# Sample attention with key pages turned in place on VectorE, all 128 score rows in use, and prompt units with one PSUM bank of each kind

## The chip, the cores and the metric

One core of a Trainium2 chip runs the whole kernel. The metric is the device time of one execution in microseconds, median of several runs. Engines are TensorE (PE), VectorE (DVE), ScalarE (ACT), GpSimd (POOL) and SyncE (SP), which issues nearly all DMAs.

## The reference, cut to what matters

The reference is one step of a two-layer decoder: a gated linear recurrence with a mixture of experts, then differential attention with a second mixture of experts, for 512 prompt tokens and 8 sequences of 4 new tokens. Only the attention of the second layer is touched. Its part for the 8 sequences, which read 16 cached pages of 128 keys each:

```python
qs = (q.astype(F32) * B_DH ** -0.5).reshape(DB, T, B_HEADS, 2, B_DH)     # 8 x 4 x 8 heads x 2 halves x 64
for p in range(n_pages):                                                  # 16 pages through page_table
    kp = cache_k[page_table[:, p]].reshape(DB, PAGE_SIZE, B_HEADS, 2, B_DH)
    vp = cache_v[page_table[:, p]]
    s = jnp.einsum('bthcd,bkhcd->bhctk', qs, kp) + alibi(p * PAGE_SIZE + jnp.arange(PAGE_SIZE))
    # running softmax over all pages and the 4 new keys, weights times vp
out = o[:, :, 0] - lam * o[:, :, 1]                                       # the two halves of a head
```

The prompt part is the same with 512 queries and keys and a causal mask: for each head and each block of 128 queries two score rows (halves c = 0, 1), a softmax of each, `a = p[:, :, 0] - lam * p[:, :, 1]`, and `a @ v`. Everything is float32. The result goes through a norm per head and the weights `b_w_o`.

## The kernel before

Layers are stages; a stage is a few blocks, in which every engine has an instruction list written out by hand, held together by semaphores. There is no scheduler: the order in the lists is the order of the code.

**kvq_block (L1575)** projects keys, queries and values from weights in `wring`, a ring of three tiles of 2 MB. Its queries are written twice, as `qT[0]` and `qT[1]`, each with the other half's 64 rows cleared (L1671, two memsets of 64x4352). SyncE loads the two halves of `b_w_o` (4.2 MB) at its end, into ring slots that nothing else then uses.

**prompt_attention (L1734)** runs 32 units, eight heads times four query blocks; unit i of a head has width 128 (i + 1). A unit is: two score matmuls (L1779), a bias with a maximum on VectorE (`bias_max`, L1831, negated in L1836), two exponentials on ScalarE (L1863), a combination with lambda on VectorE (`combine`, L1843 to L1846), transposes of the weights (L1789), their copy on ScalarE (L1871), the value matmuls (L1798), and two copies out on ScalarE (L1877, L1879). Scores, turned weights and values have two PSUM banks each (four for the scores, for two halves). TensorE works two units ahead with the scores and one behind with the values; VectorE and ScalarE work one unit ahead:

```python
bias_max(0)
for n in range(N):
    if n + 1 < N:
        bias_max(n + 1)
    combine(n)
```

GpSimd makes the bias of each head (L1769) when the one two heads before has been used. Four key pages of the first sequence are loaded meanwhile (L1730).

**sample_attention (L1894)** is a loop over the sequences: iteration b scores sequence b and takes the values of sequence b - 1. A key page (128 keys on partitions, 1024 columns of 8 heads) is turned on TensorE by eight 128x128 transposes (L2097) into two PSUM banks, ScalarE copies one bank out (L1990), VectorE the other (L2057). Four turned pages are a group of 512 keys, scored by 8 matmuls with 32 output rows each (L2115), of which 16 are in use. Values need 8 matmuls a group (L2147). The key pages have four slots in one ring tile, the value pages eight in a tile of their own; SyncE asks for a page when its slot is free. At the end of a sequence come a maximum, one exponential of 128x2052, the scaling of the weights, and `own`/`place`, which pick each head's rows and add them to the output.

**mix_out_block (L909)** then norms the output, turns it and multiplies by `b_w_o`.

## Time and profile before

| what | value |
|---|---|
| median of 3 runs | 1841.38 us (1836.94 to 1850.53) |
| the profiled execution | 1837.61 us, its span 1835.8 us |
| mean granted TensorE clock | 0.899 |
| TensorE busy | 1427.6 us (78% of the span) |
| VectorE, ScalarE, GpSimd busy | 703.8, 420.7, 151.6 us |
| read and written in DRAM | 303.37 MB and 47.84 MB |

The span is the time from the first to the last instruction in the profile; the small rest of an execution lies around it. A busy share is an average over stages with different limits, so the rows shown further down are taken by stage.

### The profile page before, as it was taken

What the parts mean: (1) busy time and instruction counts of PE and PEld (TensorE: products, weight loads), DVE (VectorE), ACT (ScalarE), POOL (GpSimd) and SP (SyncE); (2) the same over time, 40 slices, a digit from 0 to 9 for tenths busy, and PEclk for the clock granted to TensorE, in tenths of its full rate; (3) what the DMA queues carried; (4) which work ended last, traced back from release to release, by engine and by line L of the source; (5) the groups of instructions that cost most, each with busy time, mean ns of one, the idle gap of its engine ahead of it and who ended that gap; (6) DMA issues with size and microseconds to landing.
All of it is one profiled execution on the core that took longest, in us unless ns stands there. A gap on an engine that the chain in (4) does not pass through costs nothing. (4 is left out here: it accounts for less than half of the span.)

```text
span 1835.8 us, 28081 instructions
## 1 busy us (share of the span) xinstructions
PE 1427.6 (78%) x10387; PEld 816.1 (44%) x10387; DVE 703.8 (38%) x1752; ACT 420.7 (23%) x984; POOL 151.6 (8%) x174
## 2 busy tenths in 40 slices
PE   4998888986782998539989687888888769469980
PEld 2445454564441655224444454544444424245540
DVE  4225554467442111161001684344444443511115
ACT  2023343333110111030110573222222201111111
POOL 1002232222002000110000110000000000100002
PEclk9999989997895999869989898899999989679995
DMA  5133142223603999811311206999999861179974
GB/s 187 46 120 105 51 142 94 76 95 116 220 0 123 335 360 350 277 58 46 123 64 46 101 1 232 386 372 363 376 379 368 338 234 83 43 258 377 347 238 155
DMA packets 133580, 352.74 MB, mean 192 GB/s; under 512 B 22220, under 2 KB 52095, under 8 KB 125152
## 3 DMA queue, kind: packets, MB, share of 16 engines
q1 hardware_dynamic: 117108, 320.81, 48.5%
q0 software_dynamic: 4992, 17.83, 2.7%
q10 hardware_dynamic: 11372, 12.62, 2.1%
q8 instruction: 73, 1.20, 0.3%
q14 instruction: 35, 0.29, 0.0%
HBM read 303.37 MB, written 47.84 MB: 191 GB/s over the span
## 5 line engine op out<-in xcount | busy, mean ns | idle before, releaser
L431 PE MATMUL bank<-wring,xT 128*128 128x512 f32 x768 | 354.5, 622 | 22.6 <-ACT gla_fin L551 16.1
L431 PEld LDWEIGHTS bank<-wring,xT 128*128 128x128 f32 x768 | 152.1, 201 | 212.2 <-issue 192.5
L2097 PE MATMUL bank<-ident,wring 128*128 128x128 f32 x1024 | 141.9, 292 | 30.9 <-DMA wring<-cache_k 22.0
L2097 PEld LDWEIGHTS bank<-ident,wring 128*128 128x128 f32 x1024 | 122.2, 150 | 65.7 <-issue 42.5
L1990 ACT ACTIVATE sa_kT<-bank 128x512 f32<-128x512 f32 x128 | 76.5, 597 | 219.2 <-PE bank L2097 219.2
L2057 DVE COPY sa_kT<-bank 128x512 f32<-128x512 f32 x128 | 87.9, 691 | 72.5 <-PE bank L2097 72.4
L798 PE MATMUL bank<-xT,wring 128*128 128x512 f32 x256 | 111.9, 595 | 0.0
L798 PEld LDWEIGHTS bank<-xT,wring 128*128 128x128 f32 x256 | 48.1, 190 | 59.3 <-issue 59.3
L2147 PE MATMUL bank<-sa_v,sa_at 128*32 128x512 f32 x512 | 64.7, 624 | 8.5 <-DMA sa_v<-cache_v 7.1
L706 DVE COPY_PREDICATED gla_att<-level_masks,bank 128x512 f32<-128x512 int32 x48 | 35.1, 730 | 91.2 <-PE bank L818 91.2
L2115 PE MATMUL bank<-sa_kT,sa_q 128*32 128x512 f32 x512 | 62.7, 607 | 3.5 <-DVE sa_kT L2057 3.5
L2019 DVE CUSTOM_DVE_ANT_0 sa_scores<-bank,sa_alibi 128x512 f32<-128x512 f32 (+1 forms) x40 | 23.2, 580 | 93.3 <-issue 93.3
L818 PE MATMUL bank<-gla_qe,gla_ke 128*128 128x128 f32 x384 | 52.5, 295 | 4.7 <-DVE gla_att L706 4.7
L1632 PE MATMUL bank<-attn_q_xT,wring 128*128 128x512 f32 x128 | 55.7, 594 | 0.0
L322 PE MATMUL bank<-ident,attn_o 128*128 128x128 f32 (+1 forms) x80 | 11.7, 300 | 54.3 <-DVE attn_o L411 43.7
L818 PEld LDWEIGHTS bank<-gla_qe,gla_ke 128*128 128x128 f32 x384 | 49.2, 206 | 7.7 <-DVE gla_att L706 7.0
L1779 PE MATMUL bank<-attn_kT,attn_qT 128*128 128x128 f32 (+3 forms) x128 | 42.9, 462 | 10.5 <-PEq L1609 8.5
L1677 DVE COPY attn_v<-bank 128x512 f32<-128x512 f32 (+1 forms) x16 | 7.8, 488 | 96.4 <-PE bank L431 93.9
L584 ACT ACTIVATE gla_diff<-gla_diff 128x512 f32<-128x512 f32 (+1 forms) x48 | 30.3, 632 | 60.5 <-DVE gla_diff L674 51.5
L1450 PE MATMUL bank<-moe_wgu,hgrn_g 128*64 128x256 f32 x352 | 43.0, 400 | 1.2 <-DVE hgrn_g L1386 1.2
L1450 PE MATMUL bank<-moe_wgu,moe_area 128*64 128x256 f32 x352 | 42.6, 397 | 1.2 <-DVE moe_area L1386 1.2
L1435 PE MATMUL bank<-ident,hgrn_g 96*128 96x96 f32 x128 | 14.7, 261 | 36.6 <-DMA hgrn_g<-slots_x 36.6
(374 smaller groups left out, 2053.5 us busy)
## 6 DMA issues: line engine op xcount, KB each, us to landing
wring<-cache_k SPq DMA_DIRECT2D x128, 512.0 KB, 5.8
sa_v<-cache_v SPq DMA_DIRECT2D x128, 512.0 KB, 5.6
moe_wd<-moe_w_down SPq DMA_DIRECT2D x32, 1024.0 KB, 15.4
moe_wgu<-moe_w_gate SPq DMA_DIRECT2D x22, 1024.0 KB, 12.0
moe_wgu<-moe_w_up SPq DMA_DIRECT2D x22, 1024.0 KB, 13.6
wring<-a_w_in SPq DMA_DIRECT2D x16, 1024.0 KB, 8.8
slots_x<-gla_vm SPq DMA_DIRECT2D x27, 384.0 KB, 5.6
wring<-moe_w_gate SPq DMA_DIRECT2D x10, 1024.0 KB, 14.7
```

The lines of the kernel that those rows point to most:

```text
L431: last = nc.tensor.matmul(bank[:, :], xT[:, c, cols(t)], w[:, c, :], start=(c == 0), stop=(c == DC - 1))
L706: nc.vector.copy_predicated(A[:, :, :], bcast(k.levelmask[:, i, :].bitcast(I32), 1, [P, PT, P]), k.ps[3 + i % 2][:, :].rearrange("p (c n) ...
L798: last = nc.tensor.matmul(bank[:, :], lhsT, k.xT[:, c, 0:SEQ], start=(c == 0), stop=(c == DC - 1))
L818: last = nc.tensor.matmul(k.ps[3 + i % 2][:, part], KE[i][:, part], QE[i][:, part], start=True, stop=True)
L1450: nc.tensor.matmul(out, XT[u][:, c, 0:WIDE], WGU[s][:, :, c, n * P:(n + 1) * P], start=(c == 0), stop=(c == DC - 1))
L1632: last = nc.tensor.matmul(bank[:, :], w[:, c, (h % 4) * P:(h % 4 + 1) * P], q_xT[:, c, 0:SEQ], start=(c == 0), stop=(c == DC - 1))
L1779: last = nc.tensor.matmul(k.ps[2 * (n % 2) + c][:, 0:w], qT[c][:, h, i * P:(i + 1) * P], kT[:, h, 0:w], start=True, stop=True)
L1990: nc.scalar.activation(KT[:, 0:half, (p % GROUP) * P:(p % GROUP + 1) * P], k.ps[2 * (p % 2)][:, :].rearrange("p (h n) -> p h n", h=half), ...
L2057: nc.vector.tensor_copy(KT[:, half:HEADS, (p % GROUP) * P:(p % GROUP + 1) * P], k.ps[2 * (p % 2) + 1][:, :].rearrange("p (h n) -> p h n", ...
L2097: last = nc.tensor.transpose(k.ps[2 * (p % 2) + n][:, h * P:(h + 1) * P], K[:, p % KRING, hh * P:(hh + 1) * P], k.ident[:, :])
L2115: last = nc.tensor.matmul(k.ps[4][QUAD * j:QUAD * (j + 1), 0:w], Q[:, h, :], rhs, start=(n == 0), stop=(n == 1))
L2147: last = nc.tensor.matmul(k.ps[5 + n][QUAD * q:QUAD * (q + 1), :], AT[:, p, :], rhs, start=(p < 4), stop=(p == PAGES or (p >= PAGES - 3)))
```

## The change

1. **One block for both attentions.** `prompt_attention` and `sample_attention` become `attention_block` (L1754), with slots s from -32 to 36. The prompt units have the slots -32 to -1, the key groups (four pages) the slots 0 to 31, and the value group v_s = s - 5 is taken in slot s. The loops are written out; there is no loop in the instruction lists any more.
2. **Prompt units with one bank of each kind.** Two banks for the scores (one for each half), one for turned weights, one for values. In a slot TensorE does the scores of unit n + 1, then turns and values of unit n; VectorE does the combination of unit n and then the bias of n + 1. The halves are contracted over 64 rows each, so `qT` is written once and nothing of it is cleared. The division by the sum moves from the combination into ScalarE's copy of the values; the large scaling L1845 goes, a 128x1 multiply comes.
3. **Keys turned in place.** VectorE turns a page in its own SBUF tile as 4 x 32 blocks of 32x32 (STREAM_TRANSPOSE, 128x1024). A partition then holds a quarter of the keys and one of 32 features. The queries are spread to `Q`, in which each quarter of the partitions has its own eight columns, so that the 32 output rows of a matmul are four quarters x 2 halves x 4 tokens, and four matmuls over the feature chunks add up. All 128 score rows are in use, with 512 columns in two banks' halves for 16 pages. 32 matmuls of 32x128 score a group, in place of 32 transposes of 128x128 and 8 matmuls of 32x512, and the two evictions of a page go.
4. **Preparation and end of a sequence.** GpSimd clears tiles and spreads the queries (16 copies of 32x8x2x4 ahead of the first bias, 48 behind the last). TensorE spreads the queries and scores all new keys first. At the end of a sequence there are two exponentials of 128x512, some 20 small VectorE instructions that take the maximum and sum over the four quarters, and 16 small copies of the turned weights on ScalarE in place of VectorE's five reductions.
5. **Loads.** Keys and values have two groups of four pages each; the keys in two ring tiles, the values in the third and in `xT`. Key group 0 is loaded in kvq_block, group 1 at the start of attention_block. `b_w_o` moves from kvq_block to behind the last key group.

```diff
 def kvq_block(k, a, kv_xT, q_xT, ks, v, kT, qT, kTs, qs, smp_q, keys):
...
             sp.wait_ge(out_v, 2 * NT)
             store(ks, "k_prompt", "k_sample")
-            for i in range(2):
-                k.load_weights(sp, column_halves(a["b_w_o"][0], i * HB))
+            sp.wait_ge(done, count[("q", HEADS - 1)])
+            sp.wait_ge(keys.table_in, 16)
+            keys.place()
+            for p in range(GROUP):
+                keys.load_k(sp, 0, p)
...
+def attention_block(k, a, rep, v, kT, qT, kTs, qs, o_s, keys):
...
+                for s in SLOTS_S:
+                    if 1 <= s < STEPS:
+                        if s >= 2:
+                            sp.wait_ge(scored, s - 1)
+                        for r in range(GROUP):
+                            keys.load_k(sp, s, r)
+                    v_s = s - LAG
+                    if s == STEPS + 1:
+                        sp.wait_ge(scored, STEPS)
+                        for i in range(2):
+                            k.load_weights(sp, column_halves(a["b_w_o"][0], i * HB))
+                    if v_s >= 0:
+                        if v_s >= 2:
+                            sp.wait_ge(valued, v_s - 1)
+                        for r in range(GROUP):
+                            keys.load_v(sp, v_s, r)
...
+                def p_scores(n):
...
+                        if n:
+                            pe.wait_ge(p_biased, 2 * n)
+                        rows_c = slice(c * half, (c + 1) * half)
+                        nc.tensor.matmul(P_SCORE[c][:, 0:w], qT[rows_c, h, i * P:(i + 1) * P], kT[rows_c, h, 0:w],
+                                         start=True, stop=True).then_inc(p_scored, 1)
...
+                def score(s):
+                    b, g = s // GROUPS_, s % GROUPS_
+                    pe.wait_ge(keys_turned, GROUP * (s + 1))
...
+                    for n in range(2):
+                        for i in range(GROUPS_):
+                            for j in range(4):
+                                h = 2 * j + n
...
+                                last = nc.tensor.matmul(out.rearrange("p (r x) -> p r x", r=GROUP), Q[b % 2][:, h, i, :],
+                                                        keys.K[s % 2][:, :, at:at + QUAD], start=(i == 0), stop=(i == GROUPS_ - 1))
+                    last.then_inc(scored, 1)
...
+                def turn_page(s, r):
+                    dve.wait_ge(keys.k_in[s % 2 * GROUP + r], 16 * (s // 2 + 1))
+                    page = keys.K[s % 2][:, r, :]
+                    nc.vector.transpose(page, page).then_inc(keys_turned, 1)
...
+                for s in SLOTS_S:
...
+                    for n in units_at(s):
+                        p_combine(n)
+                    if 0 <= s < STEPS:
+                        turn_page(s, 0)
...
+                    for n in units_at(s + 1):
+                        p_bias_max(n)
```

In the order of VectorE's list before, in the prompt attention, the bias step of width 512 (L1831, L1836) stands ahead of the combination of width 384 (L1843 to L1846):

```order
L1831 ISA xT,pa_stat<-bank,pa_bias 128x512
L1831 ISA pa_stat 128x1
L1831 ISA xT,pa_stat<-bank,pa_bias 128x512
L1831 ISA pa_stat 128x1
L1836 TENSOR_SCALAR pa_stat<-pa_stat 128x2
L1843 RECIPROCAL pa_stat<-pa_stat 128x2
L1844 TENSOR_TENSOR pa_stat<-pa_stat,row_gains 128x1
L1845 TENSOR_SCALAR xT<-xT,pa_stat 128x384
L1846 SCALAR_TENSOR_TENSOR xT<-xT,pa_stat 128x384
```

The same engine and place now (`pa_s` holds the scores and weights, `pa_stat` the maxima and sums):

```order
L2031 RECIPROCAL pa_stat<-pa_stat 128x2
L2032 TENSOR_TENSOR pa_stat<-pa_stat 128x1
L2033 TENSOR_TENSOR pa_stat<-pa_stat,row_gains 128x1
L2034 SCALAR_TENSOR_TENSOR pa_s<-pa_s,pa_stat 128x384
L2020 ISA pa_s,pa_stat<-bank,pa_bias 128x512
L2020 ISA pa_stat 128x1
L2020 ISA pa_s,pa_stat<-bank,pa_bias 128x512
L2020 ISA pa_stat 128x1
L2024 TENSOR_SCALAR pa_stat<-pa_stat 128x2
```

The combination of the unit of width 384 now stands ahead of the bias step of the unit of width 512, which was behind it.

TensorE's list before, in the prompt attention, from the turn of the unit of width 256 on: L1779 are scores, L1789 transposes of the weights, L1798 values.

```order
L1789 MATMUL bank<-ident,xT 128x128 x2
L1798 MATMUL bank<-attn_v,pa_at 128x128
L1779 MATMUL bank<-attn_kT,attn_qT 128x128 x2
L1789 MATMUL bank<-ident,xT 128x128 x3
L1798 MATMUL bank<-attn_v,pa_at 128x128 x2
```

And now, L1876 scores, L1885 transposes, L1894 values:

```order
L1876 MATMUL bank<-attn_kT,attn_qo 128x512 x2
L1885 MATMUL bank<-ident,pa_s 128x128 x3
L1894 MATMUL bank<-attn_v,pa_at 128x128 x3
L1876 MATMUL bank<-attn_kT,attn_qo 128x128 x2
L1885 MATMUL bank<-ident,pa_s 128x128 x4
L1894 MATMUL bank<-attn_v,pa_at 128x128 x4
```

The values of a unit came one unit later than its turn; now they stand directly behind it, and the scores come one unit ahead in place of two.

## Rows read from the trace of the kernel before

**Rows 1.** The timeline of SyncE's queue: start, duration, what is issued.
```profile
1020.18 0.36 SPq L1756 DMA_DIRECT2D pa_dist<-const_dist  x1
...
1023.57 3.67 SPq L1730 DMA_DIRECT2D wring<-cache_k  x4
...
1112.71 23.02 SPq L1730 DMA_DIRECT2D wring<-cache_k  x12
...
1493.73 0.34 SPq L1242 DMA_DIRECT2D moe_norm_w<-norm_ffn_w  x1
```
**Rows 2.** Busy times by stretch: PE, PEld, DVE, ACT, POOL; clock, DMA share, GB/s.
```profile
1112.70:1484.90 372.20, 299.66 (x2334) 172.72 (x2335) 161.26 (x388) 91.36 (x141) 0.00 (x0) 0.94 0.94 357
...
1112.70:1136.50 23.80, 17.32 (x116) 11.44 (x120) 10.03 (x22) 5.38 (x9) 0.00 (x0) 0.78 0.72 242
...
1163.70:1433.50 269.80, 225.81 (x1788) 131.29 (x1787) 123.27 (x295) 70.12 (x109) 0.00 (x0) 0.96 0.98 374
...
1433.50:1449.00 15.50, 13.33 (x115) 7.25 (x112) 5.75 (x14) 3.42 (x6) 0.00 (x0) 1.00 1.01 387
...
1484.90:1493.70 8.80, 5.89 (x25) 1.24 (x25) 2.85 (x5) 0.00 (x0) 0.00 (x0) 1.00 0.00 0
```
**Rows 3.** The timeline of VectorE, prompt units: start, duration, instruction, idle time before.
```profile
1043.15 0.28 DVE L1831 CUSTOM_DVE_ANT_0 xT<-bank,pa_bias 128x128 f32<-128x128 f32 x1
...
1043.68 0.17 DVE L1836 TENSOR_SCALAR pa_stat<-pa_stat 128x2 f32<-128x2 f32 x1
...
1044.67 0.75 DVE L1846 SCALAR_TENSOR_TENSOR xT<-xT,pa_stat 128x512 f32<-128x512 f32 x1
1045.34 0.42 DVE L1831 CUSTOM_DVE_ANT_0 xT<-bank,pa_bias 128x256 f32<-128x256 f32 x1
...
1046.22 0.16 DVE L1843 RECIPROCAL pa_stat<-pa_stat 128x2 f32<-128x2 f32 x1
...
1046.61 0.29 DVE L1845 TENSOR_SCALAR xT<-xT,pa_stat 128x128 f32<-128x128 f32 x1
1046.93 0.35 DVE L1846 SCALAR_TENSOR_TENSOR xT<-xT,pa_stat 128x128 f32<-128x128 f32 x1
...
1050.14 0.69 DVE L1831 CUSTOM_DVE_ANT_0 xT<-bank,pa_bias 128x512 f32<-128x512 f32 x1
...
1051.59 0.17 DVE L1836 TENSOR_SCALAR pa_stat<-pa_stat 128x2 f32<-128x2 f32 x1
```
**Rows 4.** The timeline of ScalarE, prompt units.
```profile
1041.65 0.72 ACT L1863 ACTIVATE xT<-xT,pa_stat 128x512 f32<-128x512 f32 x1
...
1042.99 0.19 ACT L1863 ACTIVATION_READ_ACCUMULATOR xT<-xT,pa_stat 128x1 f32 x1
...
1044.74 0.40 ACT L1863 ACTIVATE xT<-xT,pa_stat 128x128 f32<-128x128 f32 x1
...
1045.41 0.19 ACT L1863 ACTIVATION_READ_ACCUMULATOR xT<-xT,pa_stat 128x1 f32 x1
...
1046.17 0.60 ACT L1871 ACTIVATE pa_at<-bank 128x512 f32<-128x512 f32 x1 [0.56 <-PE bank L1789]
```
**Rows 5.** The timeline of GpSimd, the first and a later bias of the prompt units.
```profile
1022.94 2.98 POOL L1769 TENSOR_SCALAR pa_bias<-pa_dist 128x512 f32<-128x512 f32 x2 [234.68 <-DMA pa_dist<-const_dist]
...
1061.78 1.54 POOL L1769 TENSOR_SCALAR pa_bias<-pa_dist 128x512 f32<-128x512 f32 x1 [8.60 <-DVE pa_stat L1831]
```
**Rows 6.** Groups by line: busy us and mean ns of one, idle before.
```profile
L2097 PE MATMUL bank<-ident,wring 128*128 128x128 f32 x1024 | 141.9, 292 | 30.9 <-DMA wring<-cache_k 22.0
...
L360 DVE SCALAR_TENSOR_TENSOR attn_o<-h,stat,moe_norm_w 128x1024 f32<-128x1024 f32 x5 | 10.0, 2002 | 0.2
...
L411 DVE TENSOR_SCALAR attn_o<-h,stat 128x1024 f32<-128x1024 f32 x5 | 3.6, 746 | 0.0
```
**Rows 7.** The timeline near the stream's head: the same score matmuls at two clocks.
```profile
1119.53 3.64 PE L2115 MATMUL bank<-sa_kT,sa_q 128*32 128x512 f32 x16 [0.88 <-DVE sa_kT L2057]
...
1128.26 1.93 PE L2115 MATMUL bank<-sa_kT,sa_q 128*32 128x512 f32 x16 [0.88 <-DVE sa_kT L2057]
```

More of the change, by code:

```diff
@@ L1753, in prompt_attention @@
+        (c_in, vn_in, cleared, q_spread, q_rep_ready, q_halves, q_ready, keys_turned, scored, biased, new_scored, new_biased, max_ready,
+         exped, shift_ready, shifted, sel_ready, w_turned, at_out, new_turned, new_at_out, valued, new_valued, picked, summed,
+         added) = (k.sem(f"sa_{n}") for n in names)
         with nc.Block() as block:
@@ L1756, in _ @@
                 sp.dma_start(dist[:, :], a["const_dist"]).then_inc(d_in, 16)
[L1758 to L1761 removed]
+                sp.dma_start(table[:, :], a["const_rows"][:, 2 * PAGES * QUAD:]).then_inc(c_in, 16)
+                sp.dma_start(alibi[:, :, :].rearrange("p n x -> p (n x)"), a["const_rows"][:, 0:2 * PAGES * QUAD]).then_inc(c_in, 16)
@@ L1802, in _, with spread_all_q @@
-                scores(0)
-                scores(1)
-                for n in range(N):
-                    if n + 2 < N:
-                        scores(n + 2)
-                    turn(n)
-                    if n:
-                        values(n - 1)
-                values(N - 1)
+                    last.then_inc(p_o_done, 1)
+                def spread_all_q():
+                    for i in range(GROUPS_):
+                        bank = (TURNED, VALUE[0])[i // 2]
+                        part = slice((i % 2) * HEADS * SMP, (i % 2 + 1) * HEADS * SMP)
+                        for q in range(4):
+                            last = nc.tensor.matmul(bank[QUAD * q:QUAD * (q + 1), part], k.ident[:, i * QUAD:(i + 1) * QUAD], qs[:, :, :],
+                                                    start=True, stop=True)
+                    last.then_inc(q_spread, 1)
@@ L1812, in _ @@
+                place(DEC_B - 1)
             @block.vector
@@ new lines, in add @@
+                def add(b):
+                    for n in range(2):
+                        dve.wait_ge(summed, 2 * b + n + 1)
+                        part = o_s[0:SMP, n * HB:(n + 1) * HB]
+                        nc.vector.tensor_tensor(part, part, VALUE[n][0:SMP, :], ALU.add).then_inc(added, 1)
+                nc.vector.memset(qz[:, :, :, :], 0.0).then_inc(q_halves, 1)
+                ch(nc.vector.memset(lam_row[:, 0:DEC_T], 1.0))
+                ch(nc.vector.tensor_copy(lam_row[:, DEC_T:QX], rep[:, 2 * P:2 * P + 1].to_broadcast([P, DEC_T])))
@@ L1854, in _ @@
+                pick(DEC_B - 1)
+                add(DEC_B - 1)
                 k.order_n["vector"] = ch.n
```

821 lines of the change are left out of this document (409 added, 412 removed).

## The prediction

> **What bounds the kernel now.** I read the timeline of SyncE's queue first, because it dates the stages. The prompt attention starts at 1020, the paged stream of keys and values is issued from 1112.71, and the next stage begins at 1493.73 [rows 1]. Then the busy times by stretch: in the middle of the stream, 1163.7 to 1433.5, the DMA engines are busy 0.98 of the time at 374 GB/s, and TensorE, VectorE and ScalarE are all below that (225.8, 123.3 and 70.1 of 269.8 us) [rows 2]. The reader is to see there that the stream is bound by memory, not by TensorE with its 1024 page transposes (141.9 us in the whole run, rows 6). Only its head (242 GB/s) and its tail are slower, so that 372.2 us run at 357 GB/s on average. In the prompt attention the DMA does nothing, and the kernel waits for a chain between VectorE and ScalarE, which the timelines of both engines show [rows 3, 4]. GpSimd's rows date its cadence: one bias per head, 1.54 + 8.60 = 10.14 us per head of four units [rows 5].
>
> **Part 1, the start of the stage.** Before, the first bias is computed at 1022.94, 2.7 us after the stage's start [rows 5]. Now GpSimd first clears four tiles of 1024 columns and one of 256, for which I take 4.2 us (VectorE's 1024 columns take 0.75 to 2.0 us in rows 6; GpSimd is put near the lower), and then issues 16 chained copies of 32x64 elements. The nearest row is the bias itself, 1.54 us for 512 elements [rows 5]: by elements a copy of 64 is 0.19, and it is surely under 1.54. I stay near the first and add a fixed part, 0.32 + 0.05 for the chain, so 5.9 us. First bias 4.2 + 5.9 - 2.7 = **7.4 us** later (3 to 12).
>
> **Part 2, the prompt units, one bank of each kind.** Before, VectorE does the bias step of unit n+1 ahead of the combine step of unit n, so that it lies beside ScalarE's exponentials of unit n. Now the combine comes first and the bias step behind it, and the exponentials of n+1 wait for that: exponentials, combine, bias step, exponentials form one serial chain. Its length from rows 3 and 4:
> - combine up to the next bias step: 1046.22 to 1046.93 is 0.71 us, of which the removed scaling is 0.32 (from 1046.61) and a small added multiply 0.2, so 0.59; then 0.27 (width 128) or 0.67 (width 512, 1044.67 to 1045.34). 0.86 to 1.26, mean 1.06.
> - bias step: 1043.15 to 1043.85 is 0.70, 1050.14 to 1051.76 is 1.62; mean 1.15.
> - exponentials: 1044.74 to 1045.60 is 0.86, 1041.65 to 1043.18 is 1.53; mean 1.20.
> - two hand-overs of 0.03.
> Four units make 4 x 3.47 = 13.9 us a head. Widths 256 and 384 lie between, so the mean of the ends serves. On top of that, the scores of a unit stand behind the values of the unit two before on TensorE, and these wait for ScalarE's copy (0.60 us for width 512, rows 4), which stands behind the exponentials: 0.60, four matmuls of 0.14 (141.9 us / 1024, rows 6), scores of width 256 some 0.35, together 1.5 against the 0.86 that VectorE needs. That is 0.6 once a head. A small operation that coincides with GpSimd's bias adds 0.25. 14.75, and 15.0 with a somewhat lower clock. Against 10.14: 4.86 x 8 = **38.5 us** after rounding (30 at the floor of 13.9). The 64-row scores and the dropped zero halves save TensorE work that isn't late, so I give them nothing; if that cover were gone, they would be worth under 0.3 us a unit.
>
> **Part 3, from the last unit to the stream.** Before, the first page that is not loaded ahead is issued about 7.2 us behind the last combine (a block's change and three memsets). Now two groups of four key pages are in SBUF already, and the third is issued when the first is turned and scored. What turning 128x1024 in place costs, no row shows. The nearest rows are 0.75 us for a scaling and 2.0 for a three-operand form, both of 128x1024 [rows 6]; I take 1.2: one operand, as in the first, with a margin because it is read and written in another order. Scoring is 32 matmuls of 32 output rows. Four quadrants ran together in the 16 records that took 1.93 us at 512 columns [rows 7], so 32 of 128 columns take about 1 us, 2 at the low clock. 4.8 + 1.4 = 6.2, so **-1.0**. The stream starts 7.4 + 38.5 - 1.0 = 44.9 us later.
>
> **Part 4, the stream.** It carries 120 key pages and 128 value pages of 0.524 MB (130.0 MB) and, moved in from a stretch in which the DMA had room, the two halves of b_w_o (4.2 MB): 134.2 MB. Groups are asked for two ahead on each side. When key group s lands, value group s-5 and key group s+1 are still queued, 4.2 MB or 11 us, against some 6 us to turn and score; so the queue should not run dry, in head or tail either. At 380 GB/s, between 374 of the middle and 387 of the best stretch [rows 2], 353.2 us, and 1.5 for the first landing: 354.7 against 372.2, **-17.5** (-12 to -24). The transposes, their evictions (128 on each engine) and the loop bodies that go were beside a busy DMA: nothing. VectorE's load in a batch is 16 x 1.2 + some 8.5 us of other work = 28, of 44: hidden. SyncE issues a page in 0.9 us [rows 1] and moves one in 1.4: hidden too.
>
> **Part 5, the end.** Behind the last landing 8.8 us pass before [rows 2]: values, new values, pick, place, add. The same steps stay, without a weight turn: 8.3, **-0.5**. The next stage finds its weights in SBUF and is the same, with other tile names.
>
> **Sum.** 7.4 + 38.5 - 1.0 - 17.5 - 0.5 = +26.9. The profiled execution took 1837.6 us (span 1835.8), so 1864.5. The median of the runs is 3.8 higher; I put the time between the two ways of counting, at 1866.
>
> **Two rules of the Trainium skill.** The trace shows nothing of a turn on VectorE. The Trainium skill (VectorE: DVE Perf Modes, The three transpose paths) gives 311 ns for one 128x128 in bf16; eight of these side by side would be an estimate of 2.5 us a page, against Vector Engine (DVE) Microarchitecture Reference (The reshape front-end and per-opcode configuration), by which the array sustains one element per cycle and lane. No run here shows either yet. By the second the sum stands, by the first a batch would take 48.5 us in place of 44.2, and the time would be about 1900; that is rival (b) below, which is worked out without it.
> In the stretch of loops the trace shows 374 GB/s at a share of 0.98, and 387 at its end outside the loop [rows 2]. The Trainium skill (Runtime: NRT & Kernel Launch, Instruction fetch mechanics) says that a taken branch out of the fetched pages costs a fetch; by it the unrolled stream would gain the difference, 134.2 MB at 387, 347 us and not 353.
>
> **Rivals.**
> (a) The clock falls in the prompt units. For: TensorE's work there shrinks against a longer stretch; the same 16 records took 3.64 us at the low level and 1.93 at the high one [rows 7]. Against: with waits of a microsecond between its groups the clock still stood at 0.96 in the middle of the stream [rows 2]. Values and scores double, and the chain over TensorE ends last for most widths: 17.1 us a head, 2.1 x 8 = +17, **1883**.
> (b) VectorE becomes the pace of the stream. 16 turns of t and 8.5 us reach the 44.2 us of a batch at t = 2.23 us. For: the upper bound of 2.0 is near. At twice my price, 2.4, a batch takes 46.9: 8 x 2.7 = 22, and 5 more for the first four turns, **1891**.
> (c) The chain runs at its floor and the stream at the best rate: 3 + 30 - 1 - 24 - 0.5 = +8, **1847**. For: ScalarE and VectorE hand over in 0.03 us in the rows. Against: the late scores.
> (d) The other side: the stream runs faster than any row shows, because one long queue with no TensorE reads beside it feeds it better. It has to finish in 326 us, 134.2 MB at 411 GB/s, before the kernel is no slower; at 440 it would be **1816**. Against: the engines are 0.98 to 1.0 busy at 374 to 387.
> (e) The groups don't overlap as meant and the stream pauses at each group; then the share in the middle falls, as in the head of before (242 GB/s). It lies on the side of (b), and I count it there.
>
> **How the numbers follow.** Forecast 0.56, (a) 0.13, (b) with (e) 0.08, (c) 0.17, (d) 0.06. A measurement of this kernel can tell about 1%, 18.4 us, from no change. The forecast, (a) and (b) are slower by more than that, apart from some 0.03 at the forecast's lower edge: 0.74. (c), that edge and a third of (d) lie within 1%: 0.22. Faster: 0.04. The range goes from (c), 1847, to a little over (a) together with a stream at 374 GB/s, 1893; it leaves out most of (b) and (d), and the ends of the unknown prices lie in it.
>
> **What would show it.** Right: a head's cadence of 14.5 to 15.5 us in GpSimd's biases; first stream issue near 1157; a share near 1.0 from there to the last landing, near 1512; TensorE under a third busy in it. Wrong: a cadence near 10 or 17, turns over 2.2 us, a share well below 0.98 or over 400 GB/s.

## The result and the profile after

The changed kernel takes **1931.25 us** (median of 4 runs, 1929.61 to 1936.26) against 1839.16 us of the kernel before beside it (4 runs, 1835.75 to 1850.53): ratio **1.0494**, 95% interval 1.0456 to 1.0532. It is slower, as forecast, but by 92 us and not by 27, and it lies above the range of 1847 to 1893. The profiled execution has a span of 1928.9 us against 1835.8, 93.1 more. The rows that answer to [rows 1], SyncE's queue (start, duration, what is issued; the x20 hold the second group, at 1020.05, and the next four, the first of which is issued at 1213.63):

```profile
1017.99 0.35 SPq L1806 DMA_DIRECT2D pa_dist<-const_dist  x1
...
1020.05 216.61 SPq L1735 DMA_DIRECT2D wring<-cache_k  x20
...
1583.30 0.34 SPq L1242 DMA_DIRECT2D moe_norm_w<-norm_ffn_w  x1
```

GpSimd's timeline, which answers to [rows 5] (the bracket is the idle time before and what ended it). The distance between two biases is the time of a head of four units:

```profile
1017.99 1.96 POOL L1836 MEMSET sa_q<- 128x1024 f32 x2 [231.30 <-POOLq L1609]
...
1023.25 2.26 POOL L1850 COPY sa_q<-sa_q_rep 32x64 f32<-32x64 f32 x8 [0.82 <-DVE sa_q_rep L2121]
...
1028.16 2.98 POOL L1862 TENSOR_SCALAR pa_bias<-pa_dist 128x512 f32<-128x512 f32 x2 [0.21 <-POOL sa_q L1850]
...
1111.69 1.49 POOL L1862 TENSOR_SCALAR pa_bias<-pa_dist 128x512 f32<-128x512 f32 x1 [20.85 <-DVE pa_stat L2020]
1134.47 1.49 POOL L1862 TENSOR_SCALAR pa_bias<-pa_dist 128x512 f32<-128x512 f32 x1 [21.29 <-DVE pa_stat L2020]
1157.24 1.49 POOL L1862 TENSOR_SCALAR pa_bias<-pa_dist 128x512 f32<-128x512 f32 x1 [21.29 <-DVE pa_stat L2020]
```

A head takes 22.8 us here (21.6 to 22.8 over the prompt units), where it took 10.14. Busy times by stretch, to be read against [rows 2] (PE, PEld, DVE, ACT, POOL; granted clock, DMA share, GB/s): all prompt units, one head of them, the stream from its first issue to its last landing, two parts of the stream, the end.

```profile
1028.20:1205.90 177.70, 106.17 (x350) 61.07 (x351) 67.71 (x289) 69.56 (x249) 11.86 (x8) 0.55 0.00 1
1111.70:1134.50 22.80, 13.78 (x46) 8.09 (x46) 8.49 (x37) 8.94 (x32) 1.51 (x2) 0.53 0.00 0
1213.60:1573.70 360.10, 202.45 (x2696) 113.89 (x2696) 196.99 (x358) 53.14 (x208) 11.01 (x48) 0.80 0.97 374
1253.20:1335.40 82.20, 44.94 (x620) 24.64 (x612) 45.14 (x83) 13.10 (x51) 3.67 (x16) 0.84 1.02 403
1335.40:1425.80 90.40, 53.13 (x696) 29.46 (x696) 52.41 (x94) 13.28 (x52) 3.67 (x16) 0.79 0.97 375
1573.70:1583.30 9.60, 6.94 (x24) 1.54 (x24) 2.64 (x4) 0.00 (x0) 0.00 (x0) 0.85 0.01 2
```

The same view of before, one head of its prompt units, for the clock:

```profile
1051.60:1061.70 10.10, 8.05 (x47) 5.86 (x46) 9.13 (x36) 7.94 (x34) 1.54 (x1) 1.00 0.00 1
```

| part of the span | before | after | difference | forecast |
|---|---|---|---|---|
| up to the start of the attention | 1020.2 | 1018.0 | -2.2 | 0 |
| start to first bias | 2.8 | 10.2 | +7.4 | +7.4 |
| prompt units (to the last combine's end) | 82.5 | 177.7 | **+95.2** | **+38.5** |
| last combine to first new page issue | 7.2 | 7.8 | +0.5 | -1.0 |
| stream, first issue to last landing | 372.2 | 360.1 | -12.1 | -17.5 |
| end of the stage | 8.8 | 9.6 | +0.8 | -0.5 |
| the rest of the kernel | 342.1 | 345.6 | +3.5 | 0 |

Of the 66 us that the forecast missed, 57 lie in one row, the prompt units. What a unit waits for there is seen in three timelines of after, round the unit of width 256 (ScalarE, TensorE, VectorE):

```profile
1117.09 0.40 ACT L2171 ACTIVATE pa_s<-pa_s,pa_stat 128x128 f32<-128x128 f32 x1 [0.90 <-DVE pa_stat L2024]
...
1117.87 0.57 ACT L2179 ACTIVATE pa_at<-bank 128x512 f32<-128x512 f32 x1
...
1122.92 0.51 ACT L2171 ACTIVATE pa_s<-pa_s,pa_stat 128x256 f32<-128x256 f32 x1 [1.59 <-DVE pa_stat L2024]
```

```profile
1118.50 2.08 PE L1894 MATMUL bank<-attn_v,pa_at 128*128 128x128 f32 x8 [1.29 <-ACT pa_at L2179]
1120.51 1.23 PE L1876 MATMUL bank<-attn_kT,attn_qo 64*128 64x256 f32 x4
```

```profile
1121.90 0.43 DVE L2020 CUSTOM_DVE_ANT_0 pa_s<-bank,pa_bias 128x256 f32<-128x256 f32 x1 [2.96 <-PE bank L1876]
```

ScalarE's exponentials (1117.09) hold back its copy of the turned weights (1117.87). The values of that unit wait for the copy (1118.50). The next scores stand behind them on TensorE (1120.51), the bias step waits 2.96 us for the scores (1121.90), and the next exponentials wait for the bias step (1122.92). That is 5.83 us round the loop. The four rounds of this head take 5.25, 5.83, 5.13 and 6.57 us, together 22.8, and in each of them VectorE's bias step waits for the scores (1.60, 2.96, 1.65 and 2.48 us). VectorE's combine, on which the prediction's chain rests, isn't in this loop. A score or value matmul in fp32 appears as two records here (x8 for the four value matmuls), a transpose as one.

### The profile page after: what moved, and what is told of

Same layout as the page of the kernel before. It is cut to its first block and busy times, and to the rows that moved or that the text cites. A ratio compares the mean times of both kernels' runs of the same rounds, so it can differ in the third digit from the quotient of the medians.

```text
span 1928.9 us, 28471 instructions
## 1 busy us (share of the span) xinstructions
PE 1382.1 (72%) x10955; PEld 777.0 (40%) x10955; DVE 733.5 (38%) x1726; ACT 382.5 (20%) x1038; POOL 169.0 (9%) x244
## 5 line engine op out<-in xcount | busy, mean ns | idle before, releaser
L2040 DVE STREAM_TRANSPOSE wring<-wring 128x1024 f32<-128x1024 f32 x128 | 154.5, 1227 | 73.6 <-DMA wring<-cache_k 72.7
L1931 PE MATMUL bank<-wring,sa_q 128*32 128x128 f32 x2048 | 89.5, 348 | 123.5 <-DVE wring L2040 123.5
L1931 PEld LDWEIGHTS bank<-wring,sa_q 128*32 128x32 f32 x2048 | 75.1, 142 | 156.1 <-DVE wring L2040 152.6
L1894 PE MATMUL bank<-attn_v,pa_at 128*128 128x128 f32 x160 | 44.7, 444 | 69.2 <-ACT pa_at L2179 69.2
L1894 PEld LDWEIGHTS bank<-attn_v,pa_at 128*128 128x128 f32 x160 | 35.4, 315 | 80.7 <-ACT pa_at L2179 80.7
L1965 PE MATMUL bank<-wring,sa_at 128*32 128x512 f32 x256 | 43.9, 817 | 17.6 <-DMA wring<-cache_v 17.6
L2213 ACT ACTIVATE sa_at<-bank 32x128 f32<-32x128 f32 x128 | 34.3, 268 | 92.6 <-PE bank L1965 80.7
L1876 PE MATMUL bank<-attn_kT,attn_qo 64*128 64x128 f32 (+3 forms) x128 | 45.7, 812 | 6.8 <-DVE pa_stat L2020 6.8
L2171 ACT ACTIVATE pa_s<-pa_s,pa_stat 128x128 f32<-128x128 f32 (+3 forms) x64 | 35.4, 553 | 72.3 <-DVE pa_stat L2024 72.3
L1450 PE MATMUL bank<-moe_wgu,attn_qo 128*64 128x256 f32 x352 | 42.7, 397 | 1.2 <-DVE attn_qo L1386 1.2
## 6 DMA issues: line engine op xcount, KB each, us to landing
moe_wd<-moe_w_down SPq DMA_DIRECT2D x32, 1024.0 KB, 14.8
```

Source lines behind the costliest of these rows:

```text
L1450: nc.tensor.matmul(out, XT[u][:, c, 0:WIDE], WGU[s][:, :, c, n * P:(n + 1) * P], start=(c == 0), stop=(c == DC - 1))
L1876: nc.tensor.matmul(P_SCORE[c][:, 0:w], qT[rows_c, h, i * P:(i + 1) * P], kT[rows_c, h, 0:w], start=True, stop=True).then_inc(p_scored, 1)
L1894: last = nc.tensor.matmul(P_VALUE[:, 0:P], aT[:, j, :], v[:, j, h * P:(h + 1) * P], start=(j == 0), stop=(j == i))
L1931: last = nc.tensor.matmul(out.rearrange("p (r x) -> p r x", r=GROUP), Q[b % 2][:, h, i, :], keys.K[s % 2][:, :, at:at + QUAD], start=(i == ...
L1965: last = nc.tensor.matmul(VALUE[n][QUAD * r:QUAD * (r + 1), :], AT[:, p, :], keys.V[v_s % 2][:, r, n * HB:(n + 1) * HB], start=(g == 0), s ...
L2040: nc.vector.transpose(page, page).then_inc(keys_turned, 1)
```

## The experiments

Three questions: is it the order, the banks or the clock that costs 95 us; is the turn on VectorE free; and does a version exist that beats both. Cadences are distances between two of GpSimd's biases. Each ratio is against runs of the kernel before that were taken beside the experiment (medians 1840.4, 1844.9, 1840.4 and 1840.3 us for the four groups of experiments). Experiments 1, 2, 4, 5, 6 and 8 are medians of two runs, the others of four to ten.

**1. The scores ahead of the values on TensorE.**

```diff
-                    for n in units_at(s + 1):
-                        p_scores(n)
...
                     for n in units_at(s):
                         p_turn(n)
+                    for n in units_at(s + 2):
+                        p_scores(n)
```

> The changed kernel with one thing moved: in the prompt units TensorE issues the scores of unit n+2 directly behind the turn of unit n, ahead of its values. Theory A (the chain of a unit leads from the exponentials over ScalarE's copy, the values and only then the next scores, 22.8 us a head): the scores are no longer late, a head falls to the 13.9 to 15 us of combine, bias step and exponentials, 60 to 70 us less in all, about 1865. Theory B (the low TensorE clock alone is the cause, whatever the order): the clock stays near 0.5 and a head falls by less than 3 us, over 1905. Theory C (VectorE's order, as predicted): no change, 1931.

1883.65 us, ratio 1.0203 (1.0122 to 1.0284): 48 us back by one reordering. GpSimd's biases in this run, then stretches of it (a head from 1042.97, a head from 1072.7, and two heads from 1073), then ScalarE in a later head:

```profile
1042.97 1.49 POOL L1862 TENSOR_SCALAR pa_bias<-pa_dist 128x512 f32<-128x512 f32 x1 [9.53 <-DVE pa_stat L2020]
1057.90 1.49 POOL L1862 TENSOR_SCALAR pa_bias<-pa_dist 128x512 f32<-128x512 f32 x1 [13.44 <-DVE pa_stat L2020]
```

```profile
1042.97:1057.90 14.93, 9.64 (x48) 5.81 (x48) 8.18 (x37) 8.76 (x32) 1.49 (x1) 0.89 0.00 1
1072.70:1088.40 15.70, 11.93 (x48) 7.55 (x48) 8.16 (x37) 8.72 (x32) 1.50 (x2) 0.63 0.00 0
1073.00:1103.00 30.00, 21.44 (x92) 13.29 (x90) 15.90 (x70) 17.34 (x64) 2.72 (x2) 0.72 0.00 1
```

```profile
1107.28 0.36 ACT L2186 ACTIVATE pa_s<-bank,pa_stat 128x128 f32<-128x128 f32 x1
...
1107.62 0.40 ACT L2171 ACTIVATE pa_s<-pa_s,pa_stat 128x128 f32<-128x128 f32 x1
```

A head takes 14.8 to 14.9 us at a granted clock of 0.81 to 0.89 and 15.7 at 0.63 to 0.64: with the detour gone the low clock costs under 1 us a head. The bias step now stands directly behind the combine without a wait, so what is left is the prediction's chain of exponentials, combine and bias step (mean 15.2 us a head, 15.0 forecast). TensorE isn't quite out of it: in two of the four units the exponentials (1107.62) stand in ScalarE's list behind its copies of the values (L2185, L2186), which wait for TensorE's values. In the head from 1088.4 that costs 0.7 and 0.5 us.

**2. VectorE's order of before alone** (the bias step of n+1 in front of the combine of n; one bank of each kind and TensorE's order of the changed kernel stay).

> The changed kernel with VectorE's order of before in the prompt units: the bias step of unit n+1 ahead of the combination of unit n; TensorE's order stays. Theory A: the bias step still waits for scores that stand behind the values, and the combination now waits behind it: no gain or some us lost, 1925 to 1960. Theory C (the combination ahead of the bias step is what makes the chain serial): a head falls towards 12 us, about 1850. Theory B: no change.

1961.7 us, ratio 1.0626 (1.0493 to 1.0759), 25 to 26 us a head: slower than the changed kernel by 30 us of the medians. The wait for the late scores now also stands in front of the combine (3.4 to 5.3 us in each unit of the head from 1125, against the 1.6 to 3.0 above), and the turn on TensorE waits for the combine. VectorE's order is not the cause by itself.

**3. Two banks of each kind, two buffers of turned weights, four score buffers, and all orders of before**, in the changed kernel (the banks of the sample attention are free at that time).

```diff
-    P_SCORE, P_TURNED, P_VALUE = (k.ps[4], k.ps[5]), k.ps[6], k.ps[7]
+    P_SCORE, P_TURNED, P_VALUE = ((k.ps[4], k.ps[5]), (k.ps[0], k.ps[3])), (k.ps[6], k.ps[1]), (k.ps[7], k.ps[2])
...
```

> The changed kernel with two banks of each kind for the prompt units (they use the sample side's banks, which are idle until the units end) and with the orders of before on TensorE, VectorE and ScalarE. It takes back the whole prompt part of the change. Any theory that puts the loss into the prompt units: a head takes 10.1 to 10.5 us, so 98 us less, 1830 to 1840; the rest, start +7 and stream -12, then gives a time within 5 us of before's 1839. If something else in the new block slows it (SBUF traffic, more instructions), it stays over 1850.

1845.34 us is the median of eight runs, one of which took 3553.72 us and stays unexplained; the other seven have a median of 1844.54, and the ratio is theirs: 1.0015 (0.9979 to 1.005). A head takes 10.6 us at a clock of 0.84; over the same five heads as below it is 10.8 on average, since the first is slower. The rest of the changed kernel is worth nothing net: the loss is all in the prompt units' banks, buffers and orders.

**4. Five filler matmuls behind each turn**, 128x512, results thrown away, to raise the clock.

```diff
                     for n in units_at(s):
                         p_turn(n)
+                        for _ in range(5):
+                            nc.tensor.matmul(k.ps[0][:, :], k.ident[:, :], kT[:, 0, :], start=True, stop=True)
```

> The changed kernel with five further 128x512 matmuls into an unused bank behind each turn of a prompt unit, where TensorE waits: nothing is left out, they only keep the engine busy. Theory A with both clocks: the granted clock rises from 0.53 to over 0.9 there, each link over TensorE halves, and a head goes from 22.8 to some 17 us: 1885 to 1895. Theory B alone would give the 14 to 15 us of the prediction, about 1865. If the clock is no matter, a head stays at 22.8 or grows: 1931 or more.

1950.12 us, ratio 1.0563 (1.0477 to 1.0649): this says nothing on the clock's share, since TensorE became the pace, as the stretch shows (24.00 of 24.00 us busy at a clock of 1.00).

```profile
1100.00:1124.00 24.00, 24.00 (x87) 12.22 (x86) 8.42 (x37) 8.88 (x33) 1.49 (x1) 1.00 0.00 1
```

**5. Two fillers in place of five.**

> The changed kernel with two added 128x512 fp32 matmuls behind each turn of a prompt unit, into a bank that nothing reads at that time; their results are thrown away. With five of them the granted clock was 1.00 in the prompt units but TensorE itself was busy all the time (24.05 us a head). Two take 1.5 to 1.8 us a unit at the high clock, in the time in which TensorE waits for the copy of the turned weights anyway. Theory B (the order's detour costs +3 us a head, and the low clock of 0.50 to 0.54 the other 5 to 6): if the clock goes up, 17 to 18 us a head and 1931 - 7 x 5 = about 1890 to 1900. Theory A' (the detour costs the same at either clock, waits rather than TensorE's work): 22 to 23 us a head at the high clock, 1925 to 1935. If the clock stays near 0.5 the fillers only lengthen TensorE's part: 24 us or more a head, and the run says nothing on the clock's share.

1903.14 us, ratio 1.0308 (1.0265 to 1.0351): **28 us faster than the changed kernel by adding work**. A stretch of one head, then the same places on TensorE and ScalarE as shown of after:

```profile
1060.90:1078.70 17.80, 14.81 (x63) 7.36 (x62) 8.46 (x36) 8.94 (x32) 1.49 (x1) 1.00 0.01 1
```

```profile
1084.54 1.16 PE L1894 MATMUL bank<-attn_v,pa_at 128*128 128x128 f32 x8
1085.63 0.70 PE L1876 MATMUL bank<-attn_kT,attn_qo 64*128 64x256 f32 x4
```

```profile
1083.13 0.40 ACT L2173 ACTIVATE pa_s<-pa_s,pa_stat 128x128 f32<-128x128 f32 x1 [0.59 <-DVE pa_stat L2026]
...
1087.52 0.51 ACT L2173 ACTIVATE pa_s<-pa_s,pa_stat 128x256 f32<-128x256 f32 x1 [1.06 <-DVE pa_stat L2026]
```

The loop is the same, at 4.39 us in place of 5.83: the values take 1.16 and not 2.08, the scores 0.70 and not 1.23. The fillers themselves delay nothing: the values start within 0.06 us of the end of ScalarE's copy. The clock's share is thus 22.8 - 17.8 = 5.0 us a head, and the detour at the high clock is 17.8 - 14.8 = 3.0 above experiment 1.

**6. Both reorderings** (1 and 2 together, single banks).

> The changed kernel with both reorderings at once: on TensorE the scores of unit n+2 go directly behind the turn of unit n, ahead of its values, and on VectorE the bias step of unit n+1 stands in front of unit n's combine, as in the kernel before. One bank of each kind stays. The TensorE order alone gave 14.9 to 15.75 us a head and 1883.7 us. Theory A (the scores' detour over TensorE was the whole delay; what is left is the chain combine, bias, exponentials): with the bias of n+1 beside the exponentials of n, the chain a head falls to the exponentials and the combine with the two copies of ScalarE, 12 to 13 us a head, so 7 x 2.5 = about 18 to 24 us less than 1883.7: 1860 to 1866. Rival (one bank of each kind lets nothing overlap, whatever the order): 15 us a head again, 1880 to 1887. Rival (VectorE's order hurts in itself, as it did alone, +3 us a head): 18 us a head, about 1905.

1900.06 us, ratio 1.0291 (1.0255 to 1.0327), 16.3 to 18.4 us a head: a miss for my theory, and 16 us more than with the first alone. VectorE's timeline shows why: the combine of n stands behind the bias step of n+1, that waits for the scores of n+1, and these stand behind the turn of n-1, which waits for the combine of n-1. The detour over TensorE is back in a loop:

```profile
1083.58 0.29 DVE L2020 CUSTOM_DVE_ANT_0 pa_s<-bank,pa_bias 128x128 f32<-128x128 f32 x1 [1.86 <-PE bank L1876]
...
1088.03 0.42 DVE L2020 CUSTOM_DVE_ANT_0 pa_s<-bank,pa_bias 128x256 f32<-128x256 f32 x1 [2.50 <-PE bank L1876]
```

**7. One bank of each kind, one buffer of turned weights, but all orders of before** (TensorE scores n+2, turn n, values n-1; VectorE bias n+1, combine n; ScalarE's outputs one unit later; four score buffers in place of three, the fourth in `xT`).

```diff
...
+                    for n in units_at(s + 2):
+                        p_scores(n)
+                    for n in units_at(s):
+                        p_turn(n)
+                    for n in units_at(s - 1):
+                        p_values(n)
...
```

> The changed kernel with one bank of each kind and one buffer of turned weights in the prompt units, but with all the orders of the kernel before there: TensorE scores n+2, turn n, values n-1; VectorE bias n+1, combine n; ScalarE exponentials n+1, copy of turned weights n, outputs n-1; and its ring of four score buffers. With two banks of each kind the same orders gave 10.59 us a head and 1845.3 us. Theory A (the orders do the damage: nothing that a unit waits for may stand behind another unit's detour; single banks alone cost one matmul pair a unit, since scores n+2 then wait for the bias of n+1): the chain of VectorE (10.14 a head in the kernel before) with scores at 0.35 to 1.2 us and their hand-over behind each bias, in part beside the combine: 11.5 to 13.5 us a head, 1845 + 7 x 1 to 7 x 3 = 1852 to 1867. Rival (the single banks themselves force the units one behind the other): 15 to 18 us a head, as in the runs with the single banks so far, 1880 to 1905.

1851.68 us (8 runs, 1840.0 to 1863.2), ratio 1.0046 (1.0014 to 1.0078). Its biases, the third (the first two are made together) and the last:

```profile
1041.24 1.49 POOL L1865 TENSOR_SCALAR pa_bias<-pa_dist 128x512 f32<-128x512 f32 x1 [7.93 <-DVE pa_stat L2025]
...
1095.69 1.49 POOL L1865 TENSOR_SCALAR pa_bias<-pa_dist 128x512 f32<-128x512 f32 x1 [9.61 <-DVE pa_stat L2025]
```

(1095.69 - 1041.24) / 5 = 10.9 us a head, against 10.8 of experiment 3 by the same measure, so the second banks show in no cadence; the medians differ by 7 us, with ranges that overlap. What the cadence goes with here is the clock. Two heads of this run in sequence, the first shorter than the 10.14 of the kernel before:

```profile
1062.42:1072.40 9.98, 7.54 (x48) 4.75 (x48) 8.20 (x37) 8.38 (x34) 1.49 (x1) 1.00 0.01 2
1072.40:1084.59 12.19, 10.14 (x48) 6.68 (x48) 8.21 (x37) 8.56 (x34) 1.49 (x2) 0.72 0.00 1
```

With the orders put right the single banks cost nearly nothing.

**8. The reverse: the kernel before with single banks and the changed orders** in its prompt attention, nothing else.

> The kernel before with one part of the change alone: its prompt attention with one bank of each kind (scores of both halves, turned weights, values), one buffer of turned weights, and the orders of the changed kernel on TensorE (scores n+1, turn n, values n), VectorE (combine n, bias n+1) and ScalarE (exponentials n+1, copies of n). Theory A (banks and orders in the prompt units are the whole loss, the sample attention gains a little): 22 to 24 us a head instead of 10.14, 8 x 12 = about 96 us more, 1935 to 1945. Rival (the prompt units are slow in the changed kernel because of something else in its stage, as the loads, POOL's work or one block): below 15 us a head, 1840 to 1880.

1921.18 us, ratio 1.0405 (1.0369 to 1.0442), 20.9 us a head at a clock of 0.61 to 0.83. This one part carries 76 of the 92 us; the changed kernel has a lower clock still (0.53), and 7.4 us of preparation. This run kept the four score buffers of before, as experiment 7 has them, so the fourth buffer isn't what separates 10.9 us a head from 20.9: both have single banks and four buffers, the orders differ, and experiment 3 has shown that the rest of the block makes little difference to a head. No run has the orders of before with three buffers.

**9. No turn of the key pages.** This kernel copies one column in place of the turn, so the sample scores are those of unturned keys.

```diff
-                    nc.vector.transpose(page, page).then_inc(keys_turned, 1)
+                    nc.vector.tensor_copy(page[:, 0:1], page[:, 1:2]).then_inc(keys_turned, 1)
```

> The changed kernel without the turning of the key pages: VectorE copies one column of the page in place of the 128x1024 transposition, so that the sample scores are those of unturned keys. Everything else, the waits and the semaphores too, stays. Theory (the turns are hidden behind the stream: VectorE has 25 of 43 to 45 us of work in a batch, and the stream goes at the rate of its loads): 128 turns of 1.23 us are gone but the time stays within 10 us: 8 us from the turns ahead of the first score, which have nothing to hide behind (8 in a row, 9.1 us), 0 to 2 from the last group: 1920 to 1926. Rival (key pages wait for their turn in every group, so the turn sets when a buffer comes free): one turn and a hand-over a group, 31 x 1.2 = about 37 us and the start, 1880 to 1890.

1912.7 us (1907.45 to 1919.44), ratio 1.0359 (1.0319 to 1.04): 18.5 us less by the medians, between the two expectations. The turns are not free. In the profiled executions the way from the first new page to the next stage is 13.6 us shorter (SyncE's queue of this run; the changed kernel has 1213.63 and 1583.30), and the way from the first bias to that page 2.6 us.

```profile
1212.26 22.79 SPq L1735 DMA_DIRECT2D wring<-cache_k  x16
...
1568.32 0.34 SPq L1242 DMA_DIRECT2D moe_norm_w<-norm_ffn_w  x1
```

What a turn costs in the changed kernel, by line (busy us and mean ns of one):

```profile
L2040 DVE STREAM_TRANSPOSE wring<-wring 128x1024 f32<-128x1024 f32 x128 | 154.5, 1227 | 73.6 <-DMA wring<-cache_k 72.7
```

And the stream of the run without turns, two stretches:

```profile
1287.10:1329.00 41.90, 27.05 (x360) 14.48 (x364) 9.44 (x48) 6.66 (x26) 1.85 (x8) 0.80 1.03 408
...
1369.80:1412.90 43.10, 27.56 (x348) 15.45 (x348) 9.12 (x47) 6.66 (x26) 1.85 (x8) 0.76 1.03 408
```

Without turns the DMA moves 408 GB/s all the way from 1249.5 to 1496.4. The changed kernel has 403 at first and then 375 at a share of 0.97.

**10. The turn on a scratch tile.** VectorE turns a tile of the finished prompt units in place of the page, at the same place, and the scores wait for the landings alone (unturned keys again).

> The changed kernel, where VectorE turns a scratch tile of 128x1024 (a score buffer of the finished prompt units) in place of each landed key page, at the same place in its order and behind the same landing, and where TensorE's scores wait for the landing of the four pages alone; the sample scores are those of unturned keys. VectorE's load and its memory traffic stay, and only the wait of the scores for the turn is gone. Taking the turns out altogether gave 1912.7 us, with the stream at a steady 408 GB/s; with them it was 1931.25 and 372 to 408. Theory D (the turn holds the key buffer longer, so SP issues the next group later and the DMA engines idle in between): without that wait the stream goes at 400 to 408 GB/s, 1912 to 1918. Rival (the turns' traffic slows the DMA packets themselves, or VectorE is too busy for the rest): the rate stays at 372 to 391 GB/s in most batches and the time at 1924 to 1932.

1919.89 us (1916.26 to 1927.54), ratio 1.0439 (1.0402 to 1.0477).

```profile
1331.00:1373.00 42.00, 26.77 (x351) 13.70 (x344) 25.31 (x46) 6.64 (x26) 1.83 (x8) 0.80 1.03 408
1373.00:1415.00 42.00, 26.71 (x356) 13.94 (x355) 27.13 (x47) 6.64 (x26) 1.83 (x8) 0.84 1.03 408
```

VectorE is as busy as before (some 26 us of 42), the packets aren't slowed, and the rate is 408 GB/s. So the turn takes DMA time only by holding the key buffer longer: SyncE's next group waits for the scores and these for four turns. By the medians the time is 11 of the 18.5 us better, but in the stream all 13.6 us come back, 356.3 us to the next stage against 356.1 of experiment 9:

```profile
1213.54 22.26 SPq L1735 DMA_DIRECT2D wring<-cache_k  x16
...
1569.83 0.34 SPq L1242 DMA_DIRECT2D moe_norm_w<-norm_ffn_w  x1
```

The rest of the difference lies where the two kernels do the same: in the profiled executions the attention began 3.4 us later in this run, and what follows the attention took 4.8 us longer.

Where the changed kernel loses the time is seen in what its VectorE waits for between 1300 and 1500 us (total, times, longest):

```profile
DVE attn_v L2099 <- PE bank L1972: 26.2, 4, 7.2
```

L2099 is the step that picks each head's rows at the end of a sequence. It waits for TensorE's last values, and in VectorE's list it stands between the first and the second turn of a key group. So once in a sequence three turns stand behind a wait of up to 7.2 us that they have no need of; SyncE then issues nothing for 7.3 us (1335.7 to 1343.0), and the rate falls to 260 GB/s (1343 to 1350). Experiment 9 has much the same wait (23.3 us in five times) and keeps its 408 GB/s, so it takes wait and turns together. Whether the turns would be free ahead of L2099 no run tried.

**11. The prompt units beside the stream.**

```diff
-FIRST = -len(UNITS)
+FIRST = 0
...
```

(and GpSimd spreads a sample's queries behind the bias of the same head.)

> The changed kernel with the prompt units set beside the stream instead of ahead of it: the first unit stands in the slot of the first group of key pages, so that each of the 32 units runs beside one group; POOL spreads the queries of a sample behind the bias of the same head. Nothing else changes. Per slot the stream needs 8 pages of 0.52 MB at 375 to 408 GB/s, 10.3 to 11.2 us; a unit needs 3.7 us at 14.9 a head and 5.7 at 22.8, and TensorE has 23 to 28 us of sample work and 9 to 14 of prompt work in 43 to 45. Theory (the stream's rate is the bound and hides the units): the stream starts near 1034 and ends near 1400 instead of 1574, 1931 - 170 = about 1760; range 1750 to 1810, where the upper end is for units whose waits stand in the way of the score and value groups on TensorE. Rival (the engines' in-order queues make each slot as long as its stream share plus a unit's chain): 32 x 15 = 480 us from 1034, ends at 1514, 1870.

1848.73 us (10 runs), ratio 1.0045 (1.0023 to 1.0067): 82 us less than the changed kernel, but 89 more than I had expected. In the middle the DMA is at 298 GB/s, with TensorE 138 of 200 us busy:

```profile
1150.00:1350.00 200.00, 137.76 (x1395) 80.56 (x1387) 115.94 (x281) 53.32 (x198) 13.30 (x36) 0.75 0.82 298
```

**12. The same with the TensorE order of experiment 1.**

> The interleaved kernel with the one reordering that won 48 us with the units in front: TensorE's scores of unit n+2 directly behind the turn of unit n. Theory (beside the stream a unit has 11 us for its chain, so its order does not matter): the same time as the interleaved kernel within 5 us. Rival (the wait for VectorE's bias step now stands ahead of the value group on TensorE and holds up the stream): 10 to 30 us more than the interleaved kernel without it.

**1792.62 us** (4 runs, 1788.72 to 1800.46), ratio 0.9757 (0.9712 to 0.9801): faster than both kernels. Both expectations fell, since the order won 56 us here too:

```profile
1150.00:1350.00 200.00, 138.41 (x1671) 82.08 (x1670) 138.01 (x336) 64.43 (x240) 11.81 (x35) 0.86 0.91 353
```

The same work goes through faster, and the DMA share rises from 0.82 to 0.91, the granted clock from 0.75 to 0.86. At 353 GB/s the loads still don't set the pace alone; which wait does, and how much of the 56 us is the clock, was not taken apart.

## Why the prediction was wrong

**Part 1, right.** 7.4 us later. The split was off, so the exact hit is luck: a chained copy of 32x64 took 0.28 us from start to start (0.37 taken), the memsets 4.4 us (4.2 taken), and 0.8 us went to a wait for the spread queries.

**Part 2, the step that failed.** I found both loops, but put the wrong one on the path. The serial chain of exponentials, combine and bias step was to be 13.9 us a head, and the detour over TensorE was to add "0.6 once a head". Experiment 1 confirms the first: with the detour out of the way a head takes 14.8 to 15.7. The detour was held against the combine of width 128 alone, and in the trace the bias step waits for it in all four units of a head. It was mis-sized twice.
- Its matmuls. "Four matmuls of 0.14" used the transposes of [rows 6]. The values are real fp32 products, two records each, 1.06 us for the four in the trace of before, and 1.16 in experiment 5; the scores took 0.70, not 0.35. Copy, values and scores are then 0.57 + 1.16 + 0.70 = 2.4 us at the longest and 1.7 at the shortest (experiment 5), against the 0.86 to 1.26 of the combine. The row stood in the timeline of TensorE before, at the time of [rows 3]:

```profile
1048.04 1.06 PE L1798 MATMUL bank<-attn_v,pa_at 128*128 128x128 f32 x8
```

- The clock. Rival (a) named the fall and gave it 0.13, and argued from the middle of the stream that waits of a microsecond don't lower it. There TensorE was busy 225.8 of 269.8 us [rows 2]; in the prompt units it is 13.8 of 22.8, and the granted clock is 0.53, about the lower level of 1.2 GHz. Its price was too low as well, 17.1 us a head, because it doubled matmuls that were already half of what they are.

From the runs: 4.7 (the chain, experiment 1 less before, 14.8 - 10.14), 3.0 (the detour at the high clock, experiment 5 less experiment 1) and 5.0 (the clock, after less experiment 5). As differences of neighbours they have to add up to the 12.7 of 22.8 - 10.14; the split is what they tell. The forecast had 3.8 for the chain, 0.6 for the detour, 0.25 for the clock and 0.25 for GpSimd, 4.9 in all. Its 4.86 x 8 is 38.9, not 38.5.

The prediction laid the chain to VectorE's order and put no price on TensorE's order by itself, values directly behind their turn and scores one unit ahead. Experiment 2 shows that VectorE's order alone mends nothing, and experiments 7 and 8 that the orders of all three engines together decide: with single banks a head costs 10.9 us with one set and 20.9 to 22.8 with the other.

**Part 3, nearly right.** The turn was taken at 1.2 us. Eight in a row take 9.12 us, 1.14 from start to start, and the record of one is 1.227 us on average:

```profile
1205.76 9.12 DVE L2040 STREAM_TRANSPOSE wring<-wring 128x1024 f32<-128x1024 f32 x8
```

The two rules that I had weighed: one element per cycle and lane, from the Trainium skill (Vector Engine (DVE) Microarchitecture Reference, The reshape front-end and per-opcode configuration), fits 1024 elements in 1.14 us, 1.1 ns each, though no row gives VectorE's clock; the estimate of 2.5 us a page from the Trainium skill (VectorE: DVE Perf Modes, The three transpose paths) does not hold for this form. Rival (b) falls with it. The step came out 1.5 us longer than forecast: the four turns end at 1210.3, 4.5 us behind the last combine, but the scores take 2.4 us and not 1.4, and the issue follows 0.8 us behind them.

**Part 4, the sign right, the size off by 5.** 360.1 us, -12.1 and not -17.5. The average rate of 374 GB/s hides two things against 380: the stream can do 408, and it loses that to the turns (experiments 9 and 10). The rate of 408 was no news of this kernel. The trace of before has it too, in the middle of its stream; the prediction had taken only the averages and one stretch of 387:

```profile
1400.00:1420.00 20.00, 16.55 (x135) 7.78 (x133) 8.16 (x23) 5.08 (x7) 0.00 (x0) 1.00 1.02 409
```

So a share of 0.98 was read as full, while the share at 408 GB/s is 1.02 to 1.03. "The queue should not run dry" failed: the queue was counted right, but three of four turns can stand behind a wait of VectorE, and the share fell to 0.97 in the middle. The turns cost 13.6 us of stream, where I had written "hidden". That VectorE is busy 52.4 of 90.4 us was true and wasn't the question. Rival (d), a faster stream, was half right: the rate exists, but over the whole stream only without the wait for the turns. The rule on taken branches (the Trainium skill, Runtime: NRT & Kernel Launch, Instruction fetch mechanics) was to explain 374 by the loops and 387 by their end. That reading was wrong: the key pages issued from 1433.5 to 1449 still belong to the last pass of SyncE's loop, and the row above shows 409 GB/s inside the loop. Whether a taken branch has a part in the slower stretches of before is not told apart by these runs.

**Part 5 and the rest.** The end came 0.8 longer and not 0.5 shorter. The rest of the kernel differs by 1.3 us, within what runs differ by.

## What to carry to other kernels

Where two in-order queues feed each other, write down every loop that an instruction closes and price each from the rows of the same operation and shape; the longest sets the pace, and one that is a little short at the high clock may be the longest at the low one. Before a lost buffer is blamed, try the order: here moving one group of matmuls ahead of another was worth 48 us, and the second banks, once all the orders were right, some 7 us in all. And the work of an engine that is half idle isn't hidden if it lies between a landing and the release of the buffer for the next load, the less so when something that waits stands ahead of it in the list.

## What the runs showed of the hardware

- Added TensorE work made the kernel 28 us faster. Two thrown-away matmuls a unit took the granted clock from 0.53 to 1.00, with TensorE busy 14.8 of 17.8 us in place of 13.8 of 22.8. The same value matmuls took 2.08 us at the one clock and 1.16 at the other, the same scores 1.23 and 0.70.
- The DMA engines moved 408 GB/s of 0.52 MB pages over 200 us at a share of 1.03 (experiments 9 and 10); before had 409 for 20 us and 374 on average.
- VectorE turned 128x1024 fp32 in place in blocks in 1.14 us, and such turns did not slow the packets that landed in the same memory (408 GB/s with scratch turns and without any).
